# The mixer of a two-layer decoder trunk, reordered: gate products on VectorE, taps ahead of the heads' waits, LayerNorm sums inside a chunk

## The reference, cut to what matters

```python
h = rms_norm(x, g);  z = h @ w_in + b_in
# branch A: causal depthwise convolution of 31 taps over 512 channels, then LayerNorm
a = z[A_value] * sigmoid(z[A_gate]);  a = conv31(a) + b
y_a = silu(layer_norm(a)) @ a_w_out
# branch B: 4 heads, 3 dilated causal windows each, softmax over the windows' sums
y_b = mix(attend(q, k, v)) @ b_w_out
# branch C: short convolution of 3 taps
y_c = (gb * conv3(gc * hc)) @ c_w_out
gates = sigmoid(z[G])                       # three times 1024 wide
x = x + (gates[0]*y_a + gates[1]*y_b + gates[2]*y_c) @ w_o
x = x + cross_attention(rms_norm(x), rms_norm(mem));  x = x + ffn(rms_norm(x))
```

## Time and profile before

| | us |
|---|---|
| median of 3 runs | 2011.89 |
| profiled execution: its time / its span | 2003.02 / 2001.2 |
| TensorE matmul busy | 1929.0 |
| VectorE busy | 1490.5 |
| ScalarE busy | 1214.4 |
| GpSimd busy | 122.3 |

### The profile page before, as it was taken

The page is one execution under the profiler, slowest core; times in us unless marked ns, Lnnn a source line. Parts: engine busy times, 40 slices in busy tenths (PEclk is TensorE's granted clock), DMA queues, the critical chain, the costliest instruction groups (busy, mean ns, idle before and its releaser), DMA issues.

```text
span 2001.2 us, 29649 instructions
## 1 busy us (share of the span) xinstructions
PE 1929.0 (96%) x12030; PEld 1736.2 (87%) x12030; DVE 1490.5 (74%) x1245; ACT 1214.4 (61%) x1054; POOL 122.3 (6%) x113
## 2 busy tenths in 40 slices
PE   7999899989998999899999999999999999999997
PEld 6999899989998999899878888888888888888885
DVE  5878775454446778675478888888888888888885
ACT  5445454444444445455457777777777777777774
POOL 0001230000000001320010000000000000000000
PEclk9999999999999999999999999999999999999999
DMA  7433454345454434444479999999999999999991
GB/s 287 169 135 139 148 190 173 122 148 189 168 189 155 150 137 158 148 172 166 148 305 375 346 401 372 381 380 351 386 373 382 374 371 385 346 397 376 380 385 65
DMA packets 75819, 521.37 MB, mean 261 GB/s; under 512 B 9328, under 2 KB 9812, under 8 KB 14420
## 3 DMA queue, kind: packets, MB, share of 16 engines
q1 hardware_dynamic: 72160, 508.89, 66.8%
q0 software_dynamic: 2976, 11.01, 1.9%
q10 hardware_dynamic: 596, 0.25, 0.0%
HBM read 512.77 MB, written 7.34 MB: 260 GB/s over the span
## 4 chain that ended last, share of the span: by engine, by line
PE 88%; DVE 7%; ACT 3%; issue 1%; DMA 0%; ACTq 0%; DVEq 0%; SPq 0%
PE bank L1282 27%; PE bank L1284 27%; PE bank L1283 27%; DVE wlo L848 3%; DVE U L913 2%; ACT whi L491 2%; PE bank L1638 1%; PE bank L1485 1%; PE bank L1465 1%; DVE U L864 1%; PE bank L1417 1%; DVE rstd L857 1%; PE bank L1392 1%; PE bank L1348 0%; PE bank L1360 0%
## 5 line engine op out<-in xcount | busy, mean ns | idle before, releaser
L848 DVE TENSOR_TENSOR wlo<-raw,whi 128x2048 fp32r<-128x2048 f32 x480 | 1094.7, 2287 | 347.0 <-ACT whi L491 346.7
L491 ACT ACTIVATE whi<-raw 128x2048 fp32r<-128x2048 f32 x480 | 915.4, 1910 | 249.8 <-PE bank L1284 249.8
L1282 PE MATMUL bank<-whi,act_hl 128*128 128x512 f32 (+1 forms) x1472 | 566.7, 385 | 8.9 <-DVE act_hl L1204 8.0
L1284 PE MATMUL bank<-whi,act_hl 128*128 128x512 f32 (+1 forms) x1472 | 560.1, 380 | 0.0
L1283 PE MATMUL bank<-wlo,act_hl 128*128 128x512 f32 (+1 forms) x1472 | 559.4, 380 | 0.0
L1282 PE MATMUL bank<-h_hl,whi 128*128 128x256 f32 x1632 | 468.4, 287 | 20.2 <-DVE h_hl L870 16.7
L1283 PE MATMUL bank<-h_hl,whi 128*128 128x256 f32 x1632 | 463.7, 284 | 0.0
L1284 PE MATMUL bank<-h_hl,wlo 128*128 128x256 f32 x1632 | 463.6, 284 | 0.0
L1282 PEld LDWEIGHTS bank<-h_hl,whi 128*128 128x128 f32 x1632 | 315.3, 193 | 24.6 <-issue 19.8
L1282 PEld LDWEIGHTS bank<-whi,act_hl 128*128 128x128 f32 x1472 | 276.9, 188 | 65.1 <-DVE wlo L848 14.2
L1284 PEld LDWEIGHTS bank<-whi,act_hl 128*128 128x128 f32 x1472 | 276.8, 188 | 53.5
(11 more groups left out here) (245 smaller groups left out, 1206.1 us busy)
## 6 DMA issues: line engine op xcount, KB each, us to landing
raw<-in_stream SPq DMA_DIRECT2D x476, 1024.0 KB, 6.3
raw<-in_stream SPq DMA_DIRECT2D x4, 512.0 KB, 3.6
U<-in_stream SPq DMA_DIRECT2D x2, 1024.0 KB, 9.4
U<-in_x SPq DMA_DIRECT2D x2, 512.0 KB, 5.2
memhat<-in_mem SPq DMA_DIRECT2D x1, 1024.0 KB, 17.0
memhat<-in_stream SPq DMA_DIRECT2D x1, 1024.0 KB, 7.5
hrow<-U POOLq DMA_DIRECT2D x1, 1024.0 KB, 9.9
xacc<-U POOLq DMA_DIRECT2D x1, 1024.0 KB, 10.4
```

The lines of the kernel that those rows point to most:

```text
L491: act.activation(whi[:, n % SPLIT, 0:words], src[:, 0:words], ACT.Copy).then_inc(hi_ready, 1)
L848: dve.tensor_tensor(wlo[:, n % SPLIT, 0:words], src[:, 0:words], whi[:, n % SPLIT, 0:words].bitcast(F32), ALU.subtract).then_inc(lo_ready, 1)
L1282: pe.matmul(o, st[0], mv[0], start=start, stop=False, **kw)
L1284: return pe.matmul(o, st[1], mv[0], start=False, stop=stop, **kw)
```

## The change

`PLAN` puts all four gates ahead of the outputs that they gate (`gc`, `cout`, `gb`, `bout`), and three `ga` ahead of `aout`, the last behind it. Output chunks are no longer copied by ScalarE: VectorE multiplies them from PSUM with the gate, in place (`gate_out`), and adds into `merged` (`add_out`). All GpSimd work of this kind goes, and with it `Y`, `sg` and the semaphore `product`. The taps are spread anew: up to 8 per chunk, 3 in each `post` of a head, ahead of the waits in it, none left behind chunk 27. ScalarE's `head_exp` and its LayerNorm steps run behind the split in place of ahead of it (`after_split`). The two LayerNorm sums stand half-way inside chunks 30 and 31 and write banks 5 and 6. The memory's high part is made twice: an early one in `U` at chunk 32, from which the low parts are made at 33 and 35, and the one that TensorE reads after `aout`, since `a_hi` and `a_lo` now lie where it goes.

```diff
-PLAN += [("gc", i) for i in range(4)] + [("cout", 0), ("cout", 1), ("bout", 0), ("bout", 1)]
-PLAN += [("gb", i) for i in range(4)] + [("ga", 0), ("ga", 1), ("aout", 0), ("aout", 1), ("ga", 2), ("ga", 3)]
+PLAN += [(k, i) for g, o in (("gc", "cout"), ("gb", "bout")) for k, m in ((g, 4), (o, 2)) for i in range(m)]
+PLAN += [("ga", 0), ("ga", 1), ("ga", 2), ("aout", 0), ("aout", 1), ("ga", 3)]
...
-LN_AT = (29, 31)
-MEM_AT = (34, 35)
+LN_AT = (29, 30)
+MEM_AT = (32, 33, 35)
-CONV_A_AT = dict(zip(range(3, 29), (5, 7, 7, 7, 7, 7, 7, 0, 5, 5, 0, 7, 7, 0, 1, 5, 0, 1, 2, 6, 6, 7, 7, 7, 7, 4)))
+CONV_A_AT = dict(zip(range(3, 28), (6, 8, 8, 8, 8, 8, 8, 3, 4, 6, 3, 6, 8, 3, 0, 0, 3, 0, 0, 6, 3, 5, 8, 8, 4)))
...
-            return kind(n) in ("aval", "ch", "v")
+            return kind(n) in ("aval", "ch", "v", "cout", "bout", "aout")
...
-                        if branch == 0:
-                            gp.tensor_tensor(mb, mb, yb, ALU.mult).then_inc(gated, 1)
-                        else:
-                            gp.tensor_tensor(yb, gb, yb, ALU.mult).then_inc(product, 1)
-                            gp.wait_ge(product, 8 * lay + 4 * (branch - 1) + i + 1)
-                            gp.tensor_tensor(mb, mb, yb, ALU.add).then_inc(gated, 1)
...
-                elif what in ("cout", "bout", "aout"):
-                    if what != "cout":
-                        act.wait_ge(gated, 12 * lay + (0 if what == "bout" else 4) + 2 * (i + 1))
-                    for k in range(2):
-                        ins = act.activation(Y[:, 4 * i + 2 * k:4 * i + 2 * k + 2, :],
-                                             bank[2 * (n % 2) + k][:].rearrange("p (a b) -> p a b", a=2), ACT.Copy)
-                    ins.then_inc(out_act, 1)
...
+            def after_split(n):
+                lay, c = local(n)
+                for h in range(HEADS):
+                    if c == HEAD_AT[h]:
+                        head_exp(lay, h)
+                if c == LN_AT[0]:
+                    act.wait_ge(ln_xc, lay + 1)
+                    act.activation(asq, aacc, ACT.Square).then_inc(ln_sq, 1)
+                if c == LN_AT[1]:
+                    act.wait_ge(ln_st, 2 * lay + 2)
+                    act.activation(rstd[:], bank[LN_BANK[1]][:, 0:256], ACT.Sqrt, scale=float(D) / AW,
+                                   bias=small[:, 32:33]).then_inc(ln_rt, 1)
+                if c == LN_AT[1] + 1:
+                    act.wait_ge(ln_y, lay + 1)
...
+                    act.activation(a_hi, asq, ACT.Copy).then_inc(a_hi_s, 1)
+                if c == MEM_AT[0]:
+                    for half in range(2):
+                        act.wait_ge(mf_ready, 2 * lay + half + 1)
+                        act.activation(m_early[:, 4 * half:4 * half + 4, :], hf[:, 4 * half:4 * half + 4, :],
+                                       ACT.Copy).then_inc(m_early_s, 1)
...
                     post(n - SPLIT)
                     split(n)
+                    after_split(n - SPLIT)
...
+            def gate_out(n, k):
+                what, i = PLAN[local(n)[1]]
+                to = (merged if what == "cout" else gates)[:, 4 * i + 2 * k:4 * i + 2 * k + 2, :]
+                return dve.tensor_tensor(to, bank[2 * (n % 2) + k][:].rearrange("p (a b) -> p a b", a=2), to, ALU.mult)
+
+            def add_out(pair):
+                to = merged[:, 2 * pair:2 * pair + 2, :]
+                dve.tensor_tensor(to, gates[:, 2 * pair:2 * pair + 2, :], to, ALU.add).then_inc(gated, 1)
...
+                elif what in ("cout", "bout", "aout"):
+                    gate = {"cout": "gc", "bout": "gb", "aout": "ga"}[what]
+                    alone = (what, i) == ("aout", 1)
+                    s_, val = taken(b + AT[gate, 2 if alone else 2 * i + 1])
+                    dve.wait_ge(s_, val)
+                    if not alone:
+                        mine(gate_out(n, 1))
+                    gate_out(n, 0).then_inc(out_dve, 1)
+                    if what != "cout":
+                        s_, val = taken(n)
+                        dve.wait_ge(s_, val)
+                        add_out(2 * i)
+                        if not alone:
+                            settled()
+                            add_out(2 * i + 1)
+                elif (what, i) == ("ga", 3):
+                    s_, val = taken(n)
+                    dve.wait_ge(s_, val)
+                    mine(gate_out(n - 1, 1))
+                    settled()
+                    add_out(3)
...
+                if c in HEAD_AT:
+                    conv_a_ops(lay, CONV_A_AT[c])
...
-                if c in CONV_A_AT:
+                if c in CONV_A_AT and c not in HEAD_AT:
...
-                    if c == LN_AT[0] + 1:
-                        pe.wait_ge(conv_a, KA * AB * (lay + 1))
-                        stat(aacc, AB, ln_bank(n)).then_inc(ln_st, 1)
+                    def mean_sum():
+                        pe.wait_ge(conv_a, KA * AB * (lay + 1))
+                        stat(aacc, AB, LN_BANK[0]).then_inc(ln_st, 1)
...
-                        chunk_out(n, o_hi, o_lo, 2)
+                        chunk_out(n, o_hi, o_lo, 2, mean_sum if c == LN_AT[0] + 1 else None)
+                    elif c == LN_AT[1] + 1:
+                        chunk_in(n, midway=square_sum)
```

More of the change, by code:

```diff
@@ L125, in trunk @@
         cacc, ccv, asq = u(8832, AB, S), u(8832, AB, S), u(8832, AB, S)
-        Y = u(6776, DB, S)
+        gates = u(6776, DB, S)
         prob0, prob1 = u(9856, GROUPS, P), u(9856 + 384, GROUPS, S)
@@ L593, in post @@
                 elif what in ("gb", "ga"):
[L594 to L597, removed]
+                    if what == "ga":
+                        act.wait_ge(gated, 8 * lay + i + 1)
+                    take(n, [gates[:, 2 * i + k, :] for k in range(2)], ACT.Sigmoid, lay, blk)
                 elif what in ("xk", "xq", "xv"):
@@ L621, in post @@
                     act.activation(c_hi, cacc, ACT.Copy).then_inc(c_hi_s, 1)
[L622 to L636, removed]
                 for h in range(HEADS):
@@ L645, in post @@
                     act.activation(o_hi, bank[4][:].rearrange("p (a b) -> p a b", a=2), ACT.Copy).then_inc(o_hi_s, 1)
-                if c == MEM_AT[1]:
+                if c == AT["aout", 1]:
                     for half in range(2):
-                        act.wait_ge(mf_ready, 2 * lay + half + 1)
                         act.activation(m_hi[:, 4 * half:4 * half + 4, :], hf[:, 4 * half:4 * half + 4, :],
@@ L652, in post @@
                     for pair in range(4):
-                        act.wait_ge(gated, 12 * lay + 8 + pair + 1)
+                        act.wait_ge(gated, 8 * lay + 4 + pair + 1)
                         act.activation(h_hl[:, 0, 2 * pair:2 * pair + 2, :], merged[:, 2 * pair:2 * pair + 2, :],
@@ L1009, in post @@
                     dve.wait_ge(ln_st, 2 * lay + 1)
-                    dve.scalar_tensor_tensor(aacc, bank[ln_bank(b + LN_AT[0] + 1)][:, 0:256].unsqueeze(1).to_broadcast([P, AB, S]),
+                    dve.scalar_tensor_tensor(aacc, bank[LN_BANK[0]][:, 0:256].unsqueeze(1).to_broadcast([P, AB, S]),
                                              -float(D) / AW, aacc, op0=ALU.mult, op1=ALU.add).then_inc(ln_xc, 1)
[L1012 to L1018, removed]
                 if c == OT_AT:
@@ L1029, in post @@
                         ins.then_inc(mf_ready, 1)
[L1030 to L1034, removed]
+                if c == LN_AT[1] + 1:
+                    dve.wait_ge(ln_rt, lay + 1)
+                    mine(dve.reciprocal(rstd[:], rstd[:]))
+                    settled()
+                    dve.tensor_tensor(aacc, aacc, rstd[:].unsqueeze(1).to_broadcast([P, AB, S]), ALU.mult).then_inc(ln_y, 1)
+                if c == LN_AT[1] + 2:
+                    dve.wait_ge(a_hi_s, lay + 1)
+                    dve.tensor_tensor(a_lo, asq, a_hi.bitcast(F32), ALU.subtract).then_inc(a_lo_s, 1)
+                if c in MEM_AT[1:]:
+                    half = MEM_AT.index(c) - 1
+                    dve.wait_ge(m_early_s, 2 * lay + half + 1)
+                    dve.tensor_tensor(m_lo[:, 4 * half:4 * half + 4, :], hf[:, 4 * half:4 * half + 4, :],
+                                      m_early[:, 4 * half:4 * half + 4, :].bitcast(F32), ALU.subtract).then_inc(m_lo_s, 1)
                 if c == AT["ga", 3]:
@@ L1307, in chunk_in @@
                 for o in range(2):
+                    if o and midway:
+                        midway()
                     for k in range(DB):
@@ L1339, in chunk_out @@
                 for o in range(4):
+                    if o == 2 and midway:
+                        midway()
                     for k in range(kb):
```

30 lines of the change are left out of this document (16 added, 14 removed).

## The result

The changed kernel takes **1981.37 us**, median of 4 runs (1980.21 to 1982.59); the kernel before, beside it, 2011.96 (4 runs, 2003.76 to 2012.22). The ratio is 0.9858, 95% interval 0.9832 to 0.9884. The profiled execution took 1980.26 us, its span is 1978.5, against 2003.0 and 2001.2.

What follows compares the result with a forecast made beforehand. It took TensorE as held up by late VectorE work and a serial relay, losing 11.9 us per layer. The 23.8 us in all gave 1979.2 from the profiled 2003.0, and 1988.1 from the median 2011.9; range 1975 to 2002.

Steps and rivals of the forecast that it cites:

- The sum: Second output chunk to first `wo` chunk, each layer: 78.6 us without waits in place of 90.52, a loss of 11.9.
- the same gain off it: Last step: the 23.8 us gain, taken off the shown median of 2011.9 us, gives 1988.1 us.
- The term 1.85 us per layer: First LayerNorm sum, straight after the 5.1 us wait for a VectorE tap: half clock makes it 3.7 us, not 1.85.
- The 10.8 us: 44 taps behind chunk 22: busy 28.4 us beside GpSimd against 17.6 at 0.40 each, 10.8 us per layer.
- The products from PSUM at 0.60 us: VectorE's new 12 PSUM products and 8 sums of 128x512 per layer: 0.60 us each, 12 us; upper bound 1.3 each.
- Rival (d): TensorE waits to reuse banks until VectorE has multiplied them out: slower, 2022 us at 1.95 us per instruction; chance 0.03.
- The taps placed early: 10 fewer taps behind chunk 22, 4 us per layer, moved to heads and chunks of 8: no VectorE backlog at chunk 23.
- VectorE's load: VectorE's work from second output chunk to first `wo` chunk: 72.7 us before, 68.8 of 78.6 after, so it fits.
- Rival (c): VectorE stays the bound: only its work counts, 2.8 us per layer, 5.6 in all, 2006.3 us, no change; chance 0.07.
- The walk: Step-by-step times from chunk 23 to `wo`: no wait left, slack 0.6 us at the squares, 0.8 at first `aout` chunk.
- rival (a): LayerNorm relay 2 us late: waits and half clock cost 4.4 us per layer, gain 15.0, 1996.9 us; chance 0.17.
- Rival (b): ScalarE table changes also cost a drain: low part 2.0 us late per layer, gain 19.8, 1992.1 us; chance 0.03.

## Why the prediction was right, and where not

**The sum.** Forecast 78.6 us for the stretch, measured 78.38 in both layers; forecast 11.9 us per layer, measured 12.14 and 12.22. Of these 24.4 us the span keeps 22.7. The other 1.7 us lie outside the stretch. In layer 0 it starts 0.65 us later (188.03 against 187.39), and 0.59 of that is there when the first chunk starts (22.99 against 22.40). Between the two stretches 0.9 us are lost, where the norm between the layers has a longer half-clock spell. For that norm, 44 us of before, then 44 us with nearly the same work of the changed kernel, the granted clock at 0.96 and 0.92:

```profile
596.00:640.00 44.00, 37.80 (x289) 36.83 (x289) 25.31 (x27) 21.54 (x23) 0.24 (x2) 0.96 0.41 148
```

```profile
584.00:628.00 44.00, 37.80 (x278) 36.82 (x278) 24.03 (x27) 21.53 (x23) 0.24 (x2) 0.92 0.38 148
```

The profiled execution was forecast at 1979.2 and took 1980.26.

**The median** was forecast at 1988.1 and is 1981.37. The step that failed is "the same gain off it": it takes for granted that the 8.9 us between before's profiled execution and its median stay. Nothing on record bore that out, and the changed kernel's runs lie within 2.4 us of its profiled execution. By the clocks above the 8.9 us were half-clock spells that came in some runs of before. In later sets the median of before is 2003.93 to 2004.85; beside the second set of the changed kernel (1979.62) the gain is 24.3 us, close to the forecast 23.8. The 30.6 us of the first comparison hold some 6 us of luck: three of its four runs of before took 2012 us.

**Half clock.** The term 1.85 us per layer, for the sum after the 5.1 us wait, was right. That the 2.8 us wait can bring one too was not in the sum, since the trace of before shows none there; it cost 2.6 us in layer 0 with GpSimd cut, and came up in every variant that kept a wait of 1.8 us or more in the relay, if not in each layer.

**GpSimd.** The 10.8 us that it costs the taps were right in mechanism (0.40 us each once it is silent). The products from PSUM at 0.60 us were exact (1.29 for two, the second ending its tail). Rival (d) is refuted: no bank is waited for. But its wait is not far off, as the kernels with the shorter mean sum show.

**The taps placed early.** "What they buy is a VectorE with no backlog at chunk 23" fails in its purpose: with the old table VectorE is at most some 0.6 us late, once GpSimd is silent, and nobody waits for it. The two edits cure the same wait, either is enough, and their gains can't be added.

**VectorE's load** was forecast at 68.8 us of 78.6, and is 64.9 of 79. The eight gain multiplications take 2.2 us, 0.27 each, not the 3.2 that I took from a tap (1.0 us). The other 2.9 us are low parts that GpSimd had slowed as well and the sum left alone: the memory's two took 3.7 us and take 2.4 now, the gates' took 4.1 for three and take 2.5 for four. The first error is most of why the low part has 2.2 us to spare, not 0.8. Rival (c)'s 2.8 us also leave out the 1.1 us of the multiplications that the load counts.

**The walk and rival (a).** Its order was right and its tightest place too: the squares, forecast 0.6 us to spare, measured 0.35. Rival (a) asked for 2 us of lateness, which didn't come. The danger was real: the two kernels that put a piece of the relay wrongly show what it costs, 4.3 us per layer for the sums ahead of their chunks and 8.4 for the relay ahead of the splits, where I had given 4.4. Rival (b) is refuted by the root at 230.00, and (c) by TensorE's empty wait list and an idle of 5.45 us on VectorE.

**Left open.** What decides whether a spell follows a given wait: the same wait of 2.8 us had one in layer 0 and none in layer 1 of one execution, and over the four traces that have this wait in both layers it is four with a spell and four without. Which of before's spells made up its 2011.96 in the first comparison isn't known either, since those executions have no trace. And no run makes the kernel before with the gates' new order in `PLAN` or with the relay's new places alone: that these cure the 2.8 us wait is read from what comes back when one is undone in the changed kernel.

## What to carry to other kernels

Price a stretch by what the bounding engine would need with no wait, in matmuls counted in an undisturbed window; here that gave the time to 0.2 us. Two edits that cure the same wait must not be credited twice: ask of each what is left of the wait when the other stands. And a relay across engines is decided by its order against the periodic work: half a chunk's move of a consumer was worth 4.3 us per layer, one call moved behind the periodic split 8.4, each with the half-clock spell that its wait brought.

## What the runs showed of the hardware

- A short wait of TensorE can cost more than itself. Behind one of 1.8 to 5.2 us the granted clock fell to the 1.2 GHz level, which cost some 1.8 to 3.0 us more (a stretch's surplus over 78.38 less its listed waits, which is up to 0.3 without a spell too); behind the same wait in another layer or execution it didn't.
- VectorE and GpSimd delay each other when a VectorE operation reads SBUF on two inputs beside a GpSimd one that does. One GpSimd product of 128x512 (1.3 us alone) held a VectorE instruction for up to 1.1 us, whatever its own length: a tap 0.48 to 1.55, a sum 0.69 to 1.84, a split 2.29 to 3.39; GpSimd's product took 2.0 on average there and 4.07 at most in before. `tensor_scalar` with one SBUF input was held too (0.34 to 1.46). Products with a PSUM operand (0.68) and a reciprocal (1.74) beside the same GpSimd work lost nothing.
